# Order of the attention tiles, one mask ahead and the others among its steps

## Chip, cores and metric

The kernel runs on one core of a Trainium2 chip. The metric is the device time of one execution in microseconds (us), as the median of several runs.

## What is computed

One layer of a hybrid decoder trunk on x of 1024 positions and 1024 channels, all in float32. The reference, cut to what matters here:

```python
h = rmsnorm(x, norm_g) * (1 + scale) + shift          # shift, scale, gate from c
xr, gr, q, k, v, ga, qi, ki, wi = split(h @ w_in)
y_r = rg_lru(conv(xr), ...) * silu(gr)                # recurrence, 512 channels
# attention, 8 heads of 64, in blocks of 128 queries, one shared key and value:
score = sum_h relu(qi_h . ki / 8) * wi_h / sqrt(8)    # the indexer
score = where(causal, score, -inf)
idx = top_k(score, 256)                               # keys that a query may use
p = softmax(where(in idx and causal, q . k / 8, -inf))
y_a = (p @ v) * silu(ga)
x = x + gate * (concat(y_r, y_a) @ w_out)
return rmsnorm(x, final_g)
```

## The kernel before

**Early part.** TensorE projects h in 23 tiles of w_in (each product in three passes of high and low halves), while the other engines do the recurrence and the indexer's scores. Then, for query tiles 7 to 2 (tiles 0 and 1 have no more than 256 keys), the 256th largest score of each row is sought, a bit at a time in 31 rounds. Tile i has 128 (i + 1) keys. ScalarE counts for tiles 7, 6, 5 (columns c = 0, 1, 2 of PICK), VectorE for tiles 4, 3, 2 (c = 3, 4, 5) and updates all candidates. The order of this part on each engine comes from a planner, stages(), with estimated costs; the search ends about when the last projections do.

**From search to mask.** `settle` on VectorE finishes the thresholds of c = 0, 1, 2: eight operations on three columns, a count over each of the three score rows (line 1238), and four more (to line 1245). Then `own_threshold` for c = 3, 4, 5. ScalarE compares each score row with its threshold (Sign, line 1008), in the order MASK_ORDER = 3, 4, 5, 0, 1, 2. `mask` on VectorE (lines 1253 to 1257) turns a comparison into a mask in bias_sb: find ties, a scan that ranks them, and three operations that choose and scale. Masks 3, 4, 5 are made ahead of the attention, masks 0, 1, 2 at its steps 1, 5, 9 (MASK_AT).

**Attention.** 64 steps g, one head each; the eight tiles come in the order ATT, eight steps a tile. One loop over g stands on each engine, and each engine works in its own program order:
- TensorE in step g: scores of step g (lines 1599, 1600) into PSUM pair 2 + g % 2, output pieces, at the tile's turn four transpositions of o_sb (line 1631), in odd steps the product of a pair of heads with the values (line 1643), the transpositions of the probabilities of step g-1 (line 1656), in even steps the fold (line 1665).
- VectorE: scaled scores plus mask and their row minimum into prob (line 1361), a mask where one is due, the evacuation of y (line 1375), ya_raw and ya_lo at a tile's turn (lines 1393, 1396), pt_lo of step g-1 (line 1404), o_sb of a pair (line 1418).
- ScalarE: ya_hi at the turn, pv (line 1033), pt_hi of step g-1 (line 1043), Exp of step g (line 1051), scaling and squares of finished rows (lines 1058, 1071), and wo_hi, one row block of w_out a step, from step WO_START (line 1079). yr_half makes the high half of the recurrence's output (line 1016).
- GpSimd: wo_lo (line 818), yr_lo (line 825), residual and final multiplications (lines 837 to 847).
- SyncE: loads of w_out as soon as the projections are done, then x_res and final_g, then out and in by tile.

There are three prob buffers. The minimum of step g waits for its scores and for the transpositions of step g-3.

**Output.** y of a tile is the product of its 1024 mixed channels with w_out: eight pieces a tile (line 1621, six products of 512 columns each), all into PSUM bank 3; after four pieces VectorE takes half a tile out. Piece 0 runs at step OUT_START = 20, two pieces in each of steps 20 to 26, then one a step: piece g - 13. Pieces 4k wait for the evacuation before (y_ok).

## Time and profile before

| what | value |
|---|---|
| median of 3 runs | 606.87 us (605.71 to 607.12) |
| the profiled execution: its time | 603.09 us |
| its span, first to last instruction | 601.3 us |
| TensorE busy | 531.6 us, 88% |
| VectorE busy | 429.7 us, 71% |
| ScalarE busy | 384.9 us, 64% |
| GpSimd busy | 211.3 us, 35% |
| mean granted TensorE clock | 0.949 of full speed |

The table is read from the page of the profile. Busy shares are means over stages that have different limits. PE is TensorE's products, PEld its loading of weights beside them, DVE is VectorE, ACT ScalarE, POOL GpSimd, SP SyncE. Times in rows count from the first instruction. A granted clock of 1.00 is 2.4 GHz and one of 0.50 is 1.2 GHz.

### The profile page before, as it was taken

Reading aid. Unit: us, or ns where it says so; the run is one execution under the profiler, and the core shown is the slowest. Engines: PE = TensorE matmul, PEld = TensorE weight load, DVE = VectorE, ACT = ScalarE, POOL = GpSimd, SP = SyncE. Lnnn points to the kernel's source line nnn. Section 1 sums busy time; section 2 is a strip of 40 time slices with the busy share of each in tenths; the row PEclk is TensorE's granted clock in tenths of the full one; section 3 lists DMA queues with packets and bytes.
Section 4 is the critical chain, followed back from the end, with each engine's and each line's share of the span. In section 5 each row is a group of like instructions: output and inputs, shape, how many; then the busy total and the mean of one; then the engine's idle time right before and its main releaser. Section 6 shows DMA issues by size and latency. Waiting matters only on the chain.

```text
span 601.3 us, 8070 instructions
## 1 busy us (share of the span) xinstructions
PE 531.6 (88%) x2676; PEld 441.5 (73%) x2676; DVE 429.7 (71%) x990; ACT 384.9 (64%) x683; POOL 211.3 (35%) x186
## 2 busy tenths in 40 slices
PE   0489988999999999999999527789999999999994
PEld 0467767888687777778888426678898999888873
DVE  4784659798989889997897886564566756655532
ACT  4583543554699999988897544773666665656530
POOL 6422062032345355497552000681322030413322
PEclk9999998999999999999999855599999999999998
DMA  8992393041111121134561330200201020101011
GB/s 301 396 348 77 74 293 101 23 106 35 37 35 36 37 67 38 36 106 106 131 152 35 136 144 0 92 14 2 71 1 70 1 71 1 70 1 71 1 70 71
DMA packets 19658, 51.98 MB, mean 86 GB/s; under 512 B 4128, under 2 KB 5152, under 8 KB 19616
## 3 DMA queue, kind: packets, MB, share of 16 engines
q1 hardware_dynamic: 19616, 51.45, 27.1%
q8 instruction: 22, 0.36, 0.3%
q14 instruction: 20, 0.16, 0.1%
HBM read 37.81 MB, written 4.19 MB: 70 GB/s over the span
## 4 chain that ended last, share of the span: by engine, by line
PE 69%; DVE 14%; ACT 7%; issue 5%; POOL 2%; DMA 2%; SPq 1%; DVEq 0%; POOLq 0%; ACTq 0%
PE pair L1496 26%; PE pair L1621 13%; PE pair L1643 6%; PE pair L1656 5%; PE pair L1465 4%; PE pair L1599 2%; PE pair L1573 2%; PE pair L1600 2%; PE pair L1665 2%; DVE score_sb L1325 2%; DVE rank L1254 2%; PE pair L1564 1%; PE pair L1565 1%; PE pair L1442 1%; DMA x_sb<-in_x 1%
## 5 line engine op out<-in xcount | busy, mean ns | idle before, releaser
L1404 DVE TENSOR_TENSOR pt_lo<-pair,pt_hi 128x512 fp32r<-128x512 f32 (+3 forms) x96 | 50.5, 554 | 71.7 <-ACT pt_hi L1043 71.2
L1496 PE MATMUL pair<-h_hi,w_hi 128*128 128x512 f32 x304 | 98.3, 405 | 0.0
L938 ACT ACTIVATE bias_sb<-score_sb,tinies 128x1024 bf16<-128x1024 f32 (+2 forms) x93 | 95.7, 1031 | 3.2 <-DVE tinies L1207 3.1
L1496 PE MATMUL pair<-h_lo,w_hi 128*128 128x512 f32 x304 | 94.4, 392 | 0.0
L1496 PE MATMUL pair<-h_hi,w_lo 128*128 128x512 f32 x304 | 93.7, 389 | 0.0
L1193 DVE TENSOR_SCALAR_CACHE_REDUCE bias_sb<-score_sb,tinies 128x640 bf16<-128x640 f32 (+2 forms) x93 | 72.4, 801 | 0.8
L746 POOL TENSOR_SCALAR w_hi<-w_raw 128x1024 fp32r<-128x1024 f32 (+1 forms) x22 | 23.6, 1075 | 135.0 <-DMA w_raw<-in_w_tiles 115.3
L1496 PEld LDWEIGHTS pair<-h_hi,w_hi 128*128 128x128 f32 x304 | 56.5, 189 | 14.5 <-issue 4.5
L1496 PEld LDWEIGHTS pair<-h_lo,w_hi 128*128 128x128 f32 x304 | 57.4, 189 | 12.4
L1496 PEld LDWEIGHTS pair<-h_hi,w_lo 128*128 128x128 f32 x304 | 57.3, 188 | 12.2
L1043 ACT ACTIVATE pt_hi<-pair 128x512 fp32r<-128x512 f32 (+3 forms) x96 | 43.5, 488 | 25.8 <-PE pair L1656 23.4
L837 POOL TENSOR_TENSOR x_res<-q_free,x_res 128x512 f32<-128x512 f32 x14 | 18.1, 1296 | 111.3 <-DVE q_free L1375 111.3
L955 ACT ACTIVATE relu<-pair 128x1024 f32<-128x1024 f32 (+5 forms) x48 | 34.3, 757 | 35.4 <-PE pair L1565 18.0
L1325 DVE SCALAR_TENSOR_TENSOR score_sb<-relu,tinies,score_sb 128x1024 f32<-128x1024 f32 (+5 forms) x42 | 43.5, 1077 | 7.8 <-ACT relu L955 7.8
L1656 PE MATMUL pair<-ident,prob 128*128 128x128 f32 x194 | 30.8, 287 | 18.4 <-ACT prob L1051 18.4
L1643 PE MATMUL pair<-pt_hi,v_pair 128*128 128x256 f32 x144 | 39.0, 304 | 5.0 <-DVE o_sb L1418 3.6
L1599 PE MATMUL pair<-key_hi,qs 128*128 128x512 f32 (+3 forms) x96 | 40.6, 424 | 0.0
L818 POOL TENSOR_TENSOR wo_lo<-wo_raw,wo_hi 128x1024 fp32r<-128x1024 f32 x8 | 18.7, 2364 | 59.9 <-ACT wo_hi L1079 59.9
L1656 PEld LDWEIGHTS pair<-ident,prob 128*128 128x128 f32 x194 | 23.3, 145 | 22.0 <-issue 15.8
L1033 ACT ACTIVATE pv<-pair 128x256 f32<-128x256 f32 x32 | 12.2, 380 | 39.6 <-PE pair L1643 39.5
L1643 PE MATMUL pair<-pt_lo,v_pair 128*128 128x256 f32 x144 | 37.4, 293 | 0.0
L1051 ACT ACTIVATE prob<-prob,tinies 128x256 f32<-128x256 f32 (+7 forms) x43 | 33.4, 776 | 2.8 <-DVE tinies L1361 2.8
(204 smaller groups left out, 1306.6 us busy)
## 6 DMA issues: line engine op xcount, KB each, us to landing
w_raw<-in_w_tiles SPq DMA_DIRECT2D x21, 512.0 KB, 3.8
ada<-in_ada_w SPq DMA_DIRECT2D x16, 512.0 KB, 12.1
x_sb<-in_x SPq DMA_DIRECT2D x8, 512.0 KB, 9.1
ada_g<-in_ada_w SPq DMA_DIRECT2D x8, 512.0 KB, 6.3
qs<-half_hi SPq DMA_DIRECT2D x16, 256.0 KB, 3.8
...
```

What stands on the lines that cost most here:

```text
L938: nc.scalar.activation(junk[i], score_sb[:, SCORE_OFF[i]:SCORE_OFF[i] + keys_of(i)], ACT.Sign, bias=cand[:, c:c + 1], scale=-1.0, accum_ou ...
L955: nc.scalar.activation(relu_sb[relus % 2][:, 0:n], pairs[PAIR["idx", o[1]]][:, 0:n], ACT.Relu, scale=HD ** -0.5).then_inc(slot_free, 1)
L1043: nc.scalar.activation(pt_hi[:, 4 * b:4 * b + nc4, hh, :], psum[use % 2][:, 0:nc4 * P].rearrange("p (c q) -> p c q", q=P), ACT.Copy).then_ ...
L1051: nc.scalar.activation(prob_of(g)[:, 0:n], prob_of(g)[:, 0:n], ACT.Exp, bias=negmax[:, g % 3:g % 3 + 1], scale=-1.0, accum_out=rsum[:, g % ...
L1193: nc.vector.tensor_scalar(junk[PICK[c]], scores(c), cols(c, cand), cols(c, nK), ALU.is_ge, ALU.add, accum_out=cols(c, cnt)).then_inc(count ...
L1325: nc.vector.scalar_tensor_tensor(dst, src, w, dst, ALU.mult, ALU.add).then_inc(summed, 1)
L1404: nc.vector.tensor_tensor(pt_lo[:, 4 * b:4 * b + nc4, hh, :], psum[use % 2][:, 0:nc4 * P].rearrange("p (c q) -> p c q", q=P), f32(pt_hi[:, ...
L1496: ins = nc.tensor.matmul(psum[banks[half]][0:width, :], w[b][:, k, 0:width], hh[:, k, half * HALF:(half + 1) * HALF], start=(k == 0 and p ...
L1599: nc.tensor.matmul(dst, qs[:, h, i * P:(i + 1) * P], key_hi[:, c:c + w], start=True, stop=False)
L1621: ins = nc.tensor.matmul(bank(3), y, w[:, m, half * HALF:(half + 1) * HALF], start=(m == 0 and p == 0), stop=(m == KC - 1 and p == 2))
L1643: ins = nc.tensor.matmul(psum[2][:, 0:256], v_pair[:, c, :], t[:, c, :, :].rearrange("p h q -> p (h q)"), start=(c == 0 and p == 0), stop= ...
L1656: ins = nc.tensor.transpose(psum[use % 2][:, (c % 4) * P:(c % 4 + 1) * P], prob_of(g - LAG_T)[:, c * P:(c + 1) * P], ident[:, :])
```

## The change

The tiles are taken in the order 4, 3, 2, 1, 0, 7, 6, 5. Only the mask of tile 4 is made ahead of the attention. `mask` is split into `ranks` and `biases`, and the halves stand at steps 1 and 2 (tile 3), 9 and 11 (tile 2), 16 to 21 (tiles 7, 6, 5). The settling of the thresholds of tiles 7, 6, 5 moves from before the own thresholds to steps 4 (`settle`) and 6 (`settle_counts`), and their comparisons on ScalarE to steps 8 to 10. An Exp of one element is put on ScalarE ahead of the first comparison. wo_hi starts at step 2 instead of 10, the output pieces at step 14 instead of 20 (two pieces in step 14 alone, then one a step), so the last piece stays at step 76. The prob buffers are two instead of three, and the minimum of step g waits for the transpositions of step g-2. x_res is loaded after three masks instead of six, final_g after 8 steps instead of 16. The square's by-product goes into yg, and the evacuation of y waits for the square of the tile before instead of the residual addition. Ties and ranks of tiles 7, 6, 5 lie over the scores of tile 7. Zeros for the scan and two small operands move to other PSUM banks, which brings the waits on TensorE.

```diff
-ATT = [1, 0, 4, 7, 6, 5, 3, 2]
+ATT = [4, 3, 2, 1, 0, 7, 6, 5]
...
-MASK_AT = {4 * c + 1: c for c in range(ACT_COLS)}
-WO_START = 10
-OUT_START = 20
+MASK_ORDER = (3, 4, 5, 0, 1, 2)
+RANK_AT = {1: 4, 9: 5, 16: 0, 18: 1, 20: 2}
+BIAS_AT = {2: 4, 11: 5, 17: 0, 19: 1, 21: 2}
+SETTLE_AT = (4, 6)
+CMP_AT = {8: 0, 9: 1, 10: 2}
+YR_AT = 11
+ZERO_AT = 12
+WO_START = 2
+OUT_START = 14
...
-    add("DVE", ("post",), 5.0, 4, *[("update", SEARCH_BITS - 1, c) for c in range(ACT_COLS)])
-    add("DVE", ("own_thr",), 0.3, 4, ("own", SEARCH_BITS - 1))
...
+    add("DVE", ("own_thr",), 0.3, 0, ("own", SEARCH_BITS - 1))
+    for n, c in enumerate(MASK_ORDER[:ACT_COLS]):
+        add("ACT", ("cmp", c), 0.5 + keys_of(PICK[c]) / 1200, 5, ("own_thr",), *[("cmp", b) for b in MASK_ORDER[:n]])
...
-            tie[i] = sb(f"tie{i}", R_S + 4 * SCORE_OFF[i], [P, keys_of(i)], BF16)
-            rank[i] = sb(f"rank{i}", R_S + 4 * SCORE_OFF[i] + 2 * keys_of(i), [P, keys_of(i)], F16)
+            at = R_S + 4 * SCORE_OFF[i if i in PICK[ACT_COLS:] else PICK[0]]
+            tie[i] = sb(f"tie{i}", at, [P, keys_of(i)], BF16)
+            rank[i] = sb(f"rank{i}", at + 2 * keys_of(i), [P, keys_of(i)], F16)
...
-        fg_bc = q_free[:, :, 0:P]
-        yg = [q_free[:, 4 * n:4 * n + 4, P:2 * P] for n in range(2)]
+        fg_bc = q_free[:, :, ATT[0] * P:ATT[0] * P + P]
+        yg = [q_free[:, 4 * n:4 * n + 4, ATT[1] * P:ATT[1] * P + P] for n in range(2)]
...
-            return (prob[0], prob[1], prob_late if g >= 16 else prob_early)[g % 3]
+            return prob[g % 2]
...
-            sp.wait_ge(bias_ok, len(PICK))
+            sp.wait_ge(bias_ok, len(PICK) - ACT_COLS)
...
-            sp.wait_ge(att_ps, 16)
+            sp.wait_ge(att_ps, 8)
...
+                    if o[1] == MASK_ORDER[0]:
+                        nc.scalar.activation(warm[:, :], ones[:, :], ACT.Exp)
                         act.wait_ge(own_thr_ok, 1)
...
-                if g == OUT_START - 4:
-                    act.wait_ge(bias_ok, len(PICK))
+                if g == YR_AT:
+                    act.wait_ge(bias_ok, 1)
+                    act.wait_ge(compared, len(PICK))
                     yr_half(0)
                     yr_half(1)
...
+                if g in CMP_AT:
+                    act.wait_ge(thr_ok, 2)
+                    compare(CMP_AT[g])
...
-                    nc.scalar.activation(sq_junk, x_res[ti % 2][:, half * HALF:(half + 1) * HALF], ACT.Square,
+                    xs = x_res[ti % 2][:, half * HALF:(half + 1) * HALF].rearrange("p (c q) -> p c q", q=P)
+                    nc.scalar.activation(yg[half], xs, ACT.Square,
...
+            def ranks(c):
...
+                dve.wait_ge(compared, MASK_ORDER.index(c) + 1)
+                if c < ACT_COLS:
+                    dve.wait_ge(bias_ok, MASK_ORDER.index(c))
                 link(nc.vector.tensor_scalar(tie[i][:, :], t, 0.0, None, ALU.is_equal))
+                link(nc.vector.tensor_tensor_scan(rank[i][:, :], tie[i][:, :], zero.to_broadcast([P, n]), float(n - 2 * TOPK), ALU.add, ALU.add))
+
+            def biases(c):
...
                 link(nc.vector.tensor_scalar(cols(c, nK), rank[i][:, n - 1:n], cols(c, cnt), 0.5, ALU.subtract, ALU.mult))
                 link(nc.vector.scalar_tensor_tensor(tie[i][:, :], rank[i][:, :], cols(c, nK), t, ALU.is_gt, ALU.is_gt))
                 nc.vector.tensor_scalar(t, tie[i][:, :], BIG, None, ALU.mult).then_inc(bias_ok, 1)
...
+            dve.wait_ge(evac_done, len(EVAC))
+            link(nc.vector.memset(zeros[0], 0.0))
+            ranks(MASK_ORDER[0])
+            biases(MASK_ORDER[0])
             dve.wait_ge(bias01_ok, 2)
...
-                    if g == 16:
-                        dve.wait_ge(bias_ok, len(PICK))
+                    if i in PICK and g % 8 == 0:
+                        dve.wait_ge(bias_ok, MASK_ORDER.index(PICK.index(i)) + 1)
                     dve.wait_ge(att_ps, g + 1)
-                    if g >= 3:
-
-                        dve.wait_ge(t_ps, last_t(g - 3) + 1)
+                    if g >= 2:
+                        dve.wait_ge(t_ps, last_t(g - 2) + 1)
...
-                if g in MASK_AT:
-                    mask(MASK_AT[g])
+                if g == SETTLE_AT[0]:
+                    settle()
+                if g == SETTLE_AT[1]:
+                    settle_counts()
+                if g == ZERO_AT:
+                    link(nc.vector.memset(zeros[1], 0.0))
+                if g in RANK_AT:
+                    ranks(RANK_AT[g])
+                if g in BIAS_AT:
+                    biases(BIAS_AT[g])
...
-                        dve.wait_ge(x1_ok, 2 * (ti - 1) + half + 1)
+                        dve.wait_ge(sq1_ok, 2 * (ti - 1) + half + 1)
...
+                    if g == 1:
+                        pe.wait_ge(own_thr_ok, 1)
+                    if g % 8 == 0 and i == PICK[0]:
+                        pe.wait_ge(bias_ok, len(PICK))
...
+                    if o == 0:
+                        pe.wait_ge(bias_ok, len(PICK) - ACT_COLS)
+                        pe.wait_ge(thr_ok, 2)
```

## Rows read from the trace of the kernel before

**Rows 1.** The page: granted TensorE clock in 40 slices of the span.

```profile
PEclk9999998999999999999999855599999999999998
```

**Rows 2.** Busy time by stage: window, length, then busy us (instructions) of each engine.

```profile
339.00:353.00 14.00, 0.66 (x5) 0.42 (x3) 12.33 (x28) 6.88 (x13) 0.00 (x0) 0.60 0.78 300
353.00:394.00 41.00, 28.96 (x118) 25.33 (x119) 27.67 (x82) 24.40 (x68) 12.23 (x6) 0.51 0.12 39
549.00:569.30 20.30, 19.66 (x120) 16.92 (x118) 11.41 (x35) 12.13 (x32) 6.03 (x7) 1.00 0.08 28
```

**Rows 3.** The chain that ended last: start, us, engine, tile, line.

```profile
402.03 2.85 PE pair L1621 x12
...
446.10 1.37 PE pair L1621 x6
...
449.38 0.87 PE pair L1656 x8
...
454.80 1.37 PE pair L1621 x6
...
481.44 1.66 PE pair L1643 x14
...
489.49 1.66 PE pair L1643 x14
...
588.24 5.76 PE pair L1621 x24
```

**Rows 4.** Timeline of TensorE: start, us, instruction, and the idle time before it.

```profile
355.26 0.66 PE L1656 MATMUL pair<-ident,prob 128*128 128x128 f32 x2 [15.61 <-ACT prob L1051]
```

**Rows 5.** Timeline of VectorE: settling, first masks, first minimum, a mask of 1024 keys.

```profile
338.64 1.34 DVE L1238 TENSOR_SCALAR_CACHE_REDUCE bias_sb<-score_sb,tinies 128x1024 bf16<-128x1024 f32 x1
...
342.14 0.16 DVE L1241 SCALAR_TENSOR_TENSOR tinies<-tinies 128x3 f32<-128x3 f32 x1
...
344.24 0.33 DVE L1253 TENSOR_SCALAR tie<-bias_sb 128x640 bf16<-128x640 bf16 x1 [1.08 <-ACT bias_sb L1008]
...
347.54 0.29 DVE L1253 TENSOR_SCALAR tie<-bias_sb 128x512 bf16<-128x512 bf16 x1
...
352.72 0.42 DVE L1361 CUSTOM_DVE_ANT_0 prob<-pair,bias_sb 128x256 f32<-128x256 f32 x1
...
353.40 0.42 DVE L1253 TENSOR_SCALAR tie<-bias_sb 128x1024 bf16<-128x1024 bf16 x1
...
358.09 0.42 DVE L1404 TENSOR_TENSOR pt_lo<-pair,pt_hi 128x256 fp32r<-128x256 f32 x1
```

**Rows 6.** Timeline of ScalarE: last projection, comparison, table load, two pt_hi.

```profile
339.22 1.03 ACT L919 ACTIVATE ga<-pair 128x1024 f32<-128x1024 f32 x1 [3.71 <-PE pair L1496]
343.20 0.92 ACT L1008 ACTIVATE bias_sb<-score_sb,tinies 128x640 bf16<-128x640 f32 x1 [2.95 <-DVE tinies L1221]
...
353.22 1.28 ACT L1051 ACT_TABLE_LOAD   x1 [4.17 <-DVE tinies L1361]
354.52 0.51 ACT L1051 ACTIVATE prob<-prob,tinies 128x256 f32<-128x256 f32 x1
...
394.61 0.76 ACT L1043 ACTIVATE pt_hi<-pair 128x512 fp32r<-128x512 f32 x2
...
397.00 0.77 ACT L1043 ACTIVATE pt_hi<-pair 128x512 fp32r<-128x512 f32 x2
```

**Rows 7.** Timeline of VectorE: ya_lo of two tiles.

```profile
382.32 1.26 DVE L1396 TENSOR_TENSOR ya_lo<-ya_raw,ya_hi 128x512 fp32r<-128x512 f32 x1 [0.69 <-ACT ya_hi L1027]
...
580.39 0.69 DVE L1396 TENSOR_TENSOR ya_lo<-ya_raw,ya_hi 128x512 fp32r<-128x512 f32 x1 [0.70 <-ACT ya_hi L1027]
```

**Rows 8.** Timeline of GpSimd: seven wo_lo in a row.

```profile
384.13 16.34 POOL L818 TENSOR_TENSOR wo_lo<-wo_raw,wo_hi 128x1024 fp32r<-128x1024 f32 x7 [1.09 <-ACT wo_hi L1079]
```

**Rows 9.** TensorE in two short windows: length, busy us (instructions), granted clock, DMA.

```profile
362.50:365.90 3.40, 3.26 (x15) 0.50 0.00 0
389.80:393.20 3.40, 3.40 (x13) 0.51 0.51 152
```

48 lines of the change are left out of this document (17 added, 31 removed).

## Prediction, made before the change was built

> **What bounds the kernel now.** I read the clock line of the page first, because a whole stretch of it is below full speed [rows 1]: the TensorE clock is at nines up to slice 22, at five for three slices, and at nines again. The busy shares by stage [rows 2] say what lies there. From 339 to 353 us TensorE is busy for 0.66 of 14 us and VectorE for 12.3: VectorE settles the search and makes masks. From 353 to 394 us TensorE is busy for 29.0 of 41 us at a granted clock of 0.51, that is at 1.2 of its 2.4 GHz. These are the steps of tiles 1 and 0, with hardly any work in each and no output pieces (those start at step 20). In the chain [rows 3] the first output piece runs at 402.0, the last ends at 588.24 + 5.76 = 594.0, and nearly all between is TensorE; 7.3 us of closing work follow to 601.3. So there are two regimes: until 402.0 waits and a half clock set the time, afterwards TensorE's own work does. A change is worth what it takes from the first 62 us, less what it puts into the other 192.
>
> **The start.** The first transposition runs at 355.26, after 15.61 us without work on TensorE [rows 4]. In these lie the settling, 338.64 to about 343, three masks in a row from 344.24, and the first softmax minimum at 352.72 [rows 5]; then ScalarE's table load of 1.28 us and an Exp [rows 6]. After the change the mask of tile 4 comes first, alone. The last projection is moved out of PSUM at 339.22 + 1.03 = 340.2 [rows 6] and VectorE waits for that. ScalarE then does the warming Exp: the load of 1.28 and, as an estimate, 0.2 for one element, to 341.7. From the start of a comparison of 640 keys to the start of its mask the trace has 343.20 to 344.24, 1.04; the mask takes 344.24 to 347.54, 3.3 [rows 5, 6]. The first minimum so starts at 346.0 instead of 352.7. It and the Exp are longer (640 keys, about 0.8 and 0.9, for 256 keys' 0.4 and 0.5), but the load no longer lies in the path: first transposition at 348.0, 7.3 us earlier. The Trainium skill (ScalarE: Activation LUTs, What ACT_TABLE_LOAD costs) gives 2.66 us for a switch, load and drain together. The trace has the Exp 0.02 us behind the 1.28, so I use 1.28; by the page all of this would come 1.4 us later.
>
> **Steps 0 to 13.** These steps now belong to tile 4 and most of tile 3. Prices at full clock [rows 3]: eight transpositions 0.87, so 0.109 each; fourteen products with the values 1.66, so 0.119 each. At half clock they double. Of tile 7's pair of heads (8.70, below) two pieces, sixteen transpositions and sixteen products leave 2.3 for the scores and the fold; for 640 keys I put 1.6, so 0.8 a step and 1.6 at half clock. With five transpositions (1.1) and half of a pair's ten products (1.2), one step of tile 4 is 3.9 us of TensorE at half clock.
> - Steps 0 to 2: both parts of the mask of tile 3 (2.8, on the line of the masks below) between three minima and the first waits for Exp and transposition: 7.6 us, to 353.6.
> - Steps 3 to 5: TensorE's 3.9 each, and small waits as the pipe fills, for which I allow 1.6: 13.3, to 366.9. The eight tiny settling operations at step 4 are hidden in this.
> - Step 6: the counts of the settling take 338.64 to 342.14, 3.5, and the operations behind them 0.6 [rows 5]. They stand between the minimum and pt_lo of step 5, which the values' product waits for, and behind that the transposition. Three of the tiny operations read two operands in SBUF while GpSimd makes wo_lo. For that I go by ya_lo: 1.26 while GpSimd is at work, 0.69 when it isn't [rows 7], so 0.57 each, 1.7. (A wo_lo itself takes 16.34 / 7 = 2.33 [rows 8].) With the minimum, pt_lo and o_sb (2.2) the step is 8.0, to 374.9.
> - Steps 7 to 10: ScalarE goes from one pt_hi to the next in 394.61 to 397.00, 2.39, with an Exp of 640 keys and one wo_hi in it [rows 6]. To this come the comparisons of tiles 7, 6 and 5 at steps 8 to 10 (1.2, 1.1, 1.0, in proportion to the one above), and what the half clock adds to transposition and product ahead: 3.7 each, 14.8, to 389.7.
> - Steps 11 to 13: the last mask part of tile 2 (1.1), two yr_hi, and the turn of the first tile (TensorE, VectorE, ScalarE, VectorE): 7.8. The first piece starts at 397.5, now in step 14.
>
> The third prob buffer goes for nothing: the minimum of step g needs its scores, and TensorE issues those behind the transpositions of step g-2, so the new wait is over before the old one. Nor does wo_lo hold the pieces up: with the last wo_hi at step 9 and 2.33 us for each wo_lo it is done before step 12. The earlier loads of x_res and final_g land well before step 16, where they are first read. The y evacuation waits for a square eight steps back; nothing is queued there. If that cover were gone, each would cost a square, 0.6.
>
> **From the first piece on.** Before: 402.0 to 594.0, 192.0 us. The 64 pieces are the same. The attention work left at that point isn't. A pair of heads takes 454.80 - 446.10 = 8.70 for tile 7 and 489.49 - 481.44 = 8.05 for tile 6 [rows 3], so 0.65 less for each tile down; two pieces of 1.37 come off: 4.01 for tile 4, 3.36 for tile 3, 2.06 and 1.41 for tiles 1 and 0. Before, two pairs of tile 4 and all of 7, 6, 5, 3, 2 are left. After, one pair of tile 3 and all of 2, 1, 0, 7, 6, 5. The difference is 2 x 4.01 + 3 x 3.36 - 4 x 2.06 - 4 x 1.41 = 4.2 us less. Against it, the masks of tiles 7, 6 and 5 now stand in steps 16 to 21, those of tile 2. One of 1024 keys takes 353.40 to 358.09, 4.69 [rows 5]; on the line to the 3.30 for 640 keys the other two are 4.2 and 3.8, 12.7 in all. The other work of VectorE in these steps is 11.4 in seven steps of tile 2 in the row 549.0 to 569.3 [rows 2], so 9.8 in six, and 0.7 of wait in the turn: 23.2. TensorE has 6 x 2.72 and 0.4, 16.8. VectorE becomes the bound there and adds 6.4. In these steps the y evacuation also stands behind a mask part, and the next piece needs its bank, so the pieces cannot run ahead.
>
> **Sum.** 397.5 + 192.0 - 4.2 + 6.4 = 591.7, and 7.3 behind it: 599.0 against 601.3, 2.3 us less. The profiled execution took 603.09; the runs shown have a median of 606.87, 3.8 more, so I put the same difference on that: 604.6.
>
> **The clock** is the open point of this sum. It rose at 393.2. In 389.8 to 393.2, the row ahead, TensorE was busy for all 3.40 us; in 362.5 to 365.9, where it was busy for 3.26, it didn't rise [rows 9]. After the change TensorE runs with few gaps from step 3 on and then stands for six us at step 6. I take it that the clock is at half until that stop and up again at about 383, in a stretch of products without a gap.
>
> **Rivals.**
> - *Clock up early, and through the stop.* Then steps 7 to 13 lose the extra of transposition and product, and the first piece starts at about 395.5: 2.0 less than in the sum, 4.3 less than before, 602.6. For it: tile 4 has twice the work of tile 1 in a step. Against it: six us without work ahead. 0.18.
> - *The clock stays at half until the pieces.* This is the case on the other side. Steps 10 to 13 then take 3.3 us more and the first pieces run at 1.2 GHz for 2 more: 5.3 on the sum, 3.0 slower than before, 609.9. It decides (more than 0.3% slower) when the low clock costs over 4.1, about when it lasts to the first piece. For it: the whole of 353 to 394 in the trace. 0.20.
> - *The masks hide behind the pieces.* Then the 6.4 go: 8.7 less than before, 598.2. For it: TensorE has 1.4 us more in each step than without pieces. Against it: VectorE's sum alone is over TensorE's. 0.06.
> - *VectorE is shut out while GpSimd runs.* A blocked operation then waits for the whole of a wo_lo: three times 2.33 instead of three times 0.57, 5.3 more: 3.0 slower, 609.9. For it: GpSimd gets a wo_lo in each of those steps. Against it: ya_lo lost 0.57 only. 0.08. The Trainium skill (SBUF — State Buffer, Who interferes with whom) has this rule: an operation of VectorE with two SBUF inputs and one of GpSimd that reads SBUF exclude each other for a whole instruction.
> - *Sign is not in the table that Exp uses.* Eight more loads of 1.28, 10.2: 614.8. Before, Sign ran behind Silu without a load. 0.02.
>
> **How the numbers follow.** The case of the sum has 0.46. No change within 0.3% is 1.8 us either way, about what can be told here. My step times may be off by 4 us, so of its 0.46 I give 0.24 to faster, 0.17 to same and 0.05 to slower. The early clock and the hidden masks are faster (0.24); the late clock and the shut-out are slower but for 0.04, and the tables are slower: faster 0.48, same 0.21, slower 0.31. Range: below it takes in the hidden masks' edge, 598.5; above the late clock and 1 us, 611. The likeliest case alone has 601 to 609.
>
> **What would show it.** The first minimum at 346; a table load ahead of the first comparison and none behind it; a gap of TensorE of five to six us at about 368 to 374; the first piece near 397.5 at full clock; TensorE with gaps of about 1 us a step for some 23 us behind it and VectorE full there; then pairs of 8.7 and 8.05 again in tiles 7 and 6; 7.3 us of end. I am wrong if tile 0's steps with pieces are bound by the round through ScalarE and take much over 2.1 us, or if the clock falls again.

## The result, and the profile after

The changed kernel takes 616.31 us (median of 4 runs, 611.33 to 617.34) beside 606.29 for the kernel before (4 runs, 603.57 to 607.12): ratio 1.0157, 95% interval 1.0093 to 1.0221. It is slower by about 10 us, where 604.6 was forecast. The profiled execution took 616.18 us, its span is 614.4.

The page's clock line of the kernel after, beside [rows 1]: the three fives are gone, but seven slices in a row are below nine there, where before it was four.

```profile
PEclk9879979999999999999999777678899999999998
```

Busy time by stage of the kernel after (window, length, then us and instructions of TensorE, its weight loads, VectorE, ScalarE, GpSimd, then granted clock, DMA share and GB/s):

```profile
340.00:354.50 14.50, 6.25 (x26) 5.22 (x24) 9.86 (x22) 8.95 (x20) 0.00 (x0) 0.66 0.73 290
354.50:405.80 51.30, 36.17 (x161) 31.21 (x162) 30.04 (x74) 29.59 (x62) 21.42 (x10) 0.67 0.09 31
405.80:446.10 40.30, 34.32 (x183) 29.50 (x182) 27.98 (x61) 17.48 (x44) 7.21 (x7) 0.91 0.03 12
446.10:487.10 41.00, 37.86 (x223) 31.64 (x222) 18.33 (x74) 21.54 (x71) 14.29 (x14) 1.00 0.12 41
487.10:607.10 120.00, 117.29 (x725) 102.86 (x723) 69.43 (x143) 67.50 (x139) 27.47 (x27) 1.00 0.11 40
```

The last row, tiles 7, 6 and 5, is full of TensorE's work, as everything behind the first piece was before. The first four rows, 147.1 us, hold 32.5 us in which TensorE has nothing. The head of the chain of waits (start, us, engine, tile, line):

```profile
340.00 1.03 ACT ga L916
341.04 1.28 ACT L1005
342.34 0.20 ACT tinies L1005
342.54 0.91 ACT bias_sb L943 x2
343.55 0.34 DVE tie L1262
...
347.06 0.82 DVE prob L1374
347.98 0.93 ACT prob L1050 x2
...
349.05 1.10 PE pair L1684 x4
```

The start is as forecast: the warming Exp takes its load of 1.28 us ahead of the comparison, the mask of tile 4 starts 1.01 us behind the comparison, the first minimum is at 347.06 and the first transposition at 349.05; the last two are 1.1 us later than forecast, 0.8 of it because the last projection is (340.00, not 339.22 [rows 6]). Behind the load the next operation again follows by 0.02 us, so the 2.66 us of the Trainium skill (ScalarE: Activation LUTs, What ACT_TABLE_LOAD costs) aren't seen here either.

Then it parts. Here is the timeline of VectorE, and under it that of GpSimd, of the kernel after (start, us, line, tile out<-in, idle before):

```profile
361.15 1.88 DVE L1238 TENSOR_SCALAR tinies<-tinies 128x3 int32<-128x3 int32 x1
...
373.49 1.68 DVE L1247 SCALAR_TENSOR_TENSOR tinies<-tinies 128x3 f32<-128x3 f32 x1
375.21 0.16 DVE L1248 TENSOR_TENSOR tinies<-tinies 128x3 f32<-128x3 f32 x1
...
394.98 1.37 DVE L1272 TENSOR_SCALAR bias_sb<-tie 128x384 bf16<-128x384 bf16 x1
```
```profile
360.64 4.76 POOL L815 TENSOR_TENSOR wo_lo<-wo_raw,wo_hi 128x1024 fp32r<-128x1024 f32 x2 [2.73 <-ACT wo_hi L1082]
...
370.41 4.75 POOL L815 TENSOR_TENSOR wo_lo<-wo_raw,wo_hi 128x1024 fp32r<-128x1024 f32 x2 [5.00 <-ACT wo_hi L1082]
...
394.95 2.53 POOL L822 TENSOR_TENSOR yr_lo<-yr,yr_hi 128x512 fp32r<-128x512 f32 x2 [0.56 <-ACT yr_hi L1014]
```

An operation on three columns takes 0.16 us when nothing is beside it, and 1.88 or 1.68 here. The ends tell why: 361.15 + 1.88 = 363.03, and the first of GpSimd's two instructions ends at 360.64 + 2.38 = 363.02; 373.49 + 1.68 = 375.17, and the second of the next two ends at 375.16; 394.98 + 1.37 = 396.35, and the first half of yr_lo ends at 396.22. VectorE stands until GpSimd's instruction is over. (On 384 columns the third one goes on for 0.13 us behind it; with GpSimd idle it takes 0.26.) TensorE pays for it (its timeline, idle time in brackets):

```profile
364.70 0.36 PE L1671 MATMUL pair<-pt_hi,v_pair 128*128 128x256 f32 x1 [3.17 <-DVE o_sb L1439]
...
376.91 0.55 PE L1671 MATMUL pair<-pt_hi,v_pair 128*128 128x256 f32 x1 [5.63 <-DVE o_sb L1439]
...
418.28 0.50 PE L1649 MATMUL pair<-wo_hi,yr_hi 128*128 128x512 f32 x1 [2.35 <-DVE q_free L1396]
...
435.42 0.50 PE L1649 MATMUL pair<-wo_hi,yr_hi 128*128 128x512 f32 x1 [1.91 <-DVE q_free L1396]
```

The last two are pieces that wait for the evacuation of the output half ahead, which stands behind a scan of a mask. And in tiles 1 and 0 a new wait appears, in front of ScalarE's scaling of a finished tile (timelines of GpSimd and ScalarE in step 30):

```profile
460.44 1.30 POOL L822 TENSOR_TENSOR yr_lo<-yr,yr_hi 128x512 fp32r<-128x512 f32 x1 [1.36 <-ACT yr_hi L1014]
...
462.26 0.56 POOL L840 TENSOR_TENSOR tinies<-tinies 128x1 f32<-128x1 f32 x1
```
```profile
462.85 1.15 ACT L1060 ACTIVATE x_res<-x_res,tinies 128x1024 f32<-128x1024 f32 x1 [1.45 <-POOL tinies L840]
463.90 0.36 ACT L1042 ACTIVATE pt_hi<-pair 128x256 fp32r<-128x256 f32 x1
```

ScalarE can't scale before GpSimd has the row sums, these stand behind yr_lo, and pt_hi of the next transposition stands behind the scaling: 2.6 us. This step, 30, took 3.8 us, the two ahead of it 1.7 and 2.9.

The steps of all the kernels below, each tile's eight from minimum to minimum in the profiled execution (the first tiles in the order of the change; us):

| kernel | first minimum | tile 4 | tile 3 | tile 2 | tile 1 | tile 0 | first piece | end of last piece |
|---|---|---|---|---|---|---|---|---|
| after | 347.1 | 34.7 | 32.5 | 31.8 | 21.0 | 20.0 | 405.75 | 607.1 |
| stop_split | 346.6 | 31.2 | 30.3 | 32.1 | 21.0 | 20.0 | 399.7 | 601.2 |
| hold_clock | 347.6 | 30.4 | 28.5 | 30.5 | 21.0 | 20.0 | 398.0 | 597.9 |
| wo_around | 347.4 | 28.8 | 30.4 | 31.7 | 21.0 | 20.1 | 398.05 | 599.4 |
| y_first | 348.3 | 34.7 | 31.2 | 28.6 | 20.9 | 20.0 | 404.7 | 603.8 |
| finish_later | 348.9 | 34.3 | 30.3 | 32.1 | 19.4 | 18.4 | 405.15 | 603.4 |
| heavy_all | 347.2 | 30.6 | 31.1 | 28.2 | 19.5 | 18.4 | 400.56 | 595.0 |
| heavy_around | 347.6 | 29.2 | 29.7 | 28.2 | 19.5 | 18.4 | 398.07 | 592.6 |
| heavy_tuned | 349.3 | 25.4 | 27.8 | 28.9 | 19.5 | 18.4 | 393.99 | 589.3 |

Tiles 7 and 6 take 33.3 and 33.0 in all of them, within 0.1. Each row is one profiled execution. Ratios below are to the kernel before and leave out executions more than 1.5% above a kernel's fastest, which only three kernels had, all with repeated products: 4 of 12 of before_fill (614.7 to 618.0 us), 1 of 12 of heavy_all (1046.4) and 5 of 6 of light_all (625.2 to 627.1), each at a lower mean clock than its others.

The change's own four executions span 611.33 to 617.34 us, and the interval of its ratio overlaps those of stop_split, wo_around, finish_later and y_first below. What these four gain is therefore read from their steps. But steps, too, move with the clock from one execution to the next: steps 12 and 13 took 7.4 us in the change and in masks_out, with the clock at half for 7.0 and 6.7 us of them, and 5.7 in finish_later at full clock, though its edit lies behind them.

### The profile page after: what moved, and what is told of

Same layout as the page of the kernel before. It is cut to its first block, busy times and chain, and to the rows that moved or that the text cites. A ratio compares the mean times of both kernels' runs of the same rounds, so it can differ in the third digit from the quotient of the medians.

```text
span 614.4 us, 8087 instructions
## 1 busy us (share of the span) xinstructions
PE 544.0 (89%) x2676; PEld 450.5 (73%) x2676; DVE 429.4 (70%) x991; ACT 385.5 (63%) x684; POOL 208.9 (34%) x186
## 4 chain that ended last, share of the span: by engine, by line
PE 69%; DVE 12%; ACT 8%; issue 5%; POOL 3%; DMA 2%; SPq 1%; DVEq 0%; POOLq 0%; ACTq 0%
PE pair L1517 28%; PE pair L1649 11%; PE pair L1671 7%; PE pair L1684 5%; PE pair L1486 4%; PE pair L1594 2%; PE pair L1624 2%; PE pair L1625 2%; PE pair L1585 2%; PE pair L1586 2%; DVE score_sb L1336 1%; PE pair L1693 1%; DVE rank L1263 1%; PE pair L1463 1%; ACT pt_hi L1042 1%
## 5 line engine op out<-in xcount | busy, mean ns | idle before, releaser
L1517 PEld LDWEIGHTS pair<-h_hi,w_hi 128*128 128x128 f32 x304 | 56.9, 190 | 14.8 <-issue 4.7
L1517 PEld LDWEIGHTS pair<-h_hi,w_lo 128*128 128x128 f32 x304 | 57.4, 189 | 12.3
L1042 ACT ACTIVATE pt_hi<-pair 128x512 fp32r<-128x512 f32 (+3 forms) x96 | 43.5, 488 | 28.2 <-PE pair L1684 26.6
L1684 PE MATMUL pair<-ident,prob 128*128 128x128 f32 x288 | 48.4, 301 | 13.8 <-ACT prob L1050 13.6
L960 ACT ACTIVATE relu<-pair 128x1024 f32<-128x1024 f32 (+5 forms) x48 | 34.3, 757 | 35.5 <-PE pair L1586 23.6
L1671 PE MATMUL pair<-pt_hi,v_pair 128*128 128x256 f32 x144 | 42.8, 323 | 12.4 <-DVE o_sb L1439 12.1
L1684 PEld LDWEIGHTS pair<-ident,prob 128*128 128x128 f32 x288 | 37.6, 154 | 21.1 <-ACT prob L1050 10.7
L1050 ACT ACTIVATE prob<-prob,tinies 128x640 f32<-128x640 f32 (+7 forms) x64 | 49.6, 775 | 3.0 <-DVE tinies L1374 3.0
L1374 DVE CUSTOM_DVE_ANT_0 prob<-pair,bias_sb 128x640 f32<-128x640 f32 (+7 forms) x64 | 47.9, 749 | 0.8 <-PE pair L1625 0.4
L1671 PEld LDWEIGHTS pair<-pt_hi,v_pair 128*128 128x128 f32 x144 | 31.5, 219 | 16.0 <-DVE pt_lo L1425 15.4
L1671 PE MATMUL pair<-pt_lo,v_pair 128*128 128x256 f32 x144 | 41.4, 314 | 0.0
```

The source lines that it names most:

```text
L1042: nc.scalar.activation(pt_hi[:, 4 * b:4 * b + nc4, hh, :], psum[use % 2][:, 0:nc4 * P].rearrange("p (c q) -> p c q", q=P), ACT.Copy).then_ ...
L1050: nc.scalar.activation(prob_of(g)[:, 0:n], prob_of(g)[:, 0:n], ACT.Exp, bias=negmax[:, g % 3:g % 3 + 1], scale=-1.0, accum_out=rsum[:, g % ...
L1374: nc.vector.tensor_tensor_reduce(out=prob_of(g)[:, 0:n], in0=pairs[2 + g % 2][:, 0:n], in1=bias_sb[:, BIAS_OFF[i]:BIAS_OFF[i] + n], scale= ...
L1517: ins = nc.tensor.matmul(psum[banks[half]][0:width, :], w[b][:, k, 0:width], hh[:, k, half * HALF:(half + 1) * HALF], start=(k == 0 and p ...
L1671: ins = nc.tensor.matmul(psum[2][:, 0:256], v_pair[:, c, :], t[:, c, :, :].rearrange("p h q -> p (h q)"), start=(c == 0 and p == 0), stop= ...
L1684: ins = nc.tensor.transpose(psum[use % 2][:, (c % 4) * P:(c % 4 + 1) * P], prob_of(g - LAG_T)[:, c * P:(c + 1) * P], ident[:, :])
```

## The experiments

**Masks left out (masks_out).** The ranks and biases of tiles 7, 6 and 5 are left out; these tiles use the raw comparison as bias.

```
                 if g in RANK_AT:
-                    ranks(RANK_AT[g])
+                    if RANK_AT[g] >= ACT_COLS: ranks(RANK_AT[g])
                 if g in BIAS_AT:
-                    biases(BIAS_AT[g])
+                    if BIAS_AT[g] >= ACT_COLS: biases(BIAS_AT[g])
+                    else: (two memsets of one column, the second counting bias_ok)
```

> The changed kernel without the mask work of tiles 7, 6 and 5: ranks and biases of these are left out at steps 16 to 21, so these tiles use what the comparison left. Theory masks: the eight steps of tile 2 took 31.8 us where before they took about 23; they fall to 23, and 8 to 9 us go, to about 608. Theory that only what goes beyond TensorE's work counts (6.4 as predicted): about 610. If the clock's falls in these steps are what costs, they are gone too and 10 us or more go.

Measured 607.03 us, ratio 1.0021 (0.9995 to 1.0046). Tile 2's steps fall from 31.8 to 22.9 us, all else stays. The three masks cost 8.9 us beside TensorE's pieces; I had forecast 6.4. In the change the clock also falls to half twice in these steps, for 3.4 us each (419.7 and 436.8), and in masks_out it doesn't: what that costs is within the 8.9.

**One count a step (stop_split).** The settling is put at step 3, its three counts at steps 4, 5 and 6.

```
-SETTLE_AT = (4, 6)
+SETTLE_AT = (3, 4)
-                for c in range(ACT_COLS):
+                for c in (g - SETTLE_AT[1],):
+                if c < ACT_COLS - 1: return
```

> The changed kernel with the settling at step 3 and its three counts one each at steps 4, 5 and 6, with the closing operations behind the third. Theory stop (a single block of 4 us on VectorE makes TensorE idle for 5.6 and lets the clock fall): 3 to 5 us go, to about 612. Theory sum (VectorE's work in the head counts, wherever it stands): no change within 1 us, 616.

Measured 611.48 us, ratio 1.0111 (1.0079 to 1.0142); the first piece comes at 399.7, 6 us earlier. But step 6, now with one count in place of three, still took 7.1 us (7.4): the operations behind the counts took 1.62 and 2.35 us there. So 2.4 us of counts went out of step 6, and 2.1 us of standing beside GpSimd came in. The gain lies elsewhere: 3.3 us in steps 3 to 5, and 1.7 in steps 12 and 13, where its clock was at full. These 1.7 are in finish_later too, so they are not the split's.

**The clock held (hold_clock).** Score products are repeated to the same place, so that TensorE isn't idle.

```
+FILL_AT = {1: 10, 3: 1, 5: 4, 7: 7, 9: 1, 11: 4, 13: 2}
-                    for c in range(0, n, HALF):
+                    for c in [*range(0, n, HALF)] * (1 + FILL_AT.get(g, 0)):
```

> The changed kernel with the score products of steps 1, 3, 5, 7, 9, 11 and 13 repeated (10, 1, 4, 7, 1, 4, 2 times more, the same result), so that TensorE is at work where it stood idle. Theory clock: the granted clock stays at 1.0 from 341 to the first piece, transpositions and products halve there, and the first piece comes 5 to 8 us earlier: about 609. Theory rounds (the head is bound by VectorE and ScalarE): the clock is at 1.0, but no more than 2 us go.

Measured 608.94 us, ratio 1.0064 (1.0035 to 1.0092). The row of hold_clock from its first minimum to its first piece, and under it that of after, both with the clock in the third column from the end:

```profile
347.60:398.00 50.40, 38.27 (x247) 32.45 (x246) 36.73 (x88) 33.02 (x70) 21.62 (x10) 1.00 0.19 71
```
```profile
347.10:405.80 58.70, 41.15 (x179) 35.45 (x180) 36.55 (x88) 33.63 (x71) 21.42 (x10) 0.65 0.16 60
```

At full clock the stretch is 8.3 us shorter, although TensorE gets 68 instructions more, as the theory of the clock had it.

**The same in the kernel before (before_fill).**

```
+FILL_AT = {1: 60, 2: 2, 3: 5, 4: 2, 5: 4, 6: 2, 7: 5, 8: 4, 9: 3, 10: 4, 11: 7, 12: 8, 13: 4, 14: 4, 15: 4}
```

> The kernel before with the score products of its steps 1 to 15 repeated (the same operands to the same place; 60 extra times at step 1, where TensorE is idle 15.6 us, 2 to 8 times at the others), and nothing else. Theory A (the half clock of 342.2 to 393.2 is a cost of the light tiles: their transpositions, folds and products lie in the round of a step and take 0.25 to 0.45 us more in it): the granted clock stays 1.0 from 342 to the end, the 16 light steps fall from 38.4 to about 33 us, the whole to 600. Theory B (the light steps are bound by VectorE and ScalarE and the clock costs nothing there): the steps stay at 38 and the whole within 0.3% of the kernel before, or above it by what the repeats add.

Measured ratio 0.9993 (0.9967 to 1.0018). The row of its sixteen light steps:

```profile
354.60:392.20 37.60, 30.55 (x233) 28.56 (x231) 26.74 (x77) 20.64 (x61) 8.32 (x4) 0.95 0.08 29
```

The clock was at 0.95 in place of 0.51 [rows 2], and the steps took 37.6 us in place of 38.4. My expectation of 33 was wrong. But the repeats were in the way too. In the timeline of VectorE minima wait for the repeated products (line 1601), here the three longest of five:

```profile
356.00 0.42 DVE L1362 CUSTOM_DVE_ANT_0 prob<-pair,bias_sb 128x256 f32<-128x256 f32 x1 [0.94 <-PE pair L1601]
...
364.71 0.42 DVE L1362 CUSTOM_DVE_ANT_0 prob<-pair,bias_sb 128x256 f32<-128x256 f32 x1 [0.38 <-PE pair L1601]
...
367.32 0.42 DVE L1362 CUSTOM_DVE_ANT_0 prob_early<-pair,bias_sb 128x256 f32<-128x256 f32 x1 [0.94 <-PE pair L1601]
```

These waits are 2.6 us in all; in the kernel before none of the sixteen minima waits for TensorE, and in hold_clock one does, for 0.28. So under tiles 1 and 0 the half clock costs 0.8 us as measured, and by my estimate up to 3.4, if all these waits hid a gain; under tiles 4 and 3 the low clock costs over 8.

**Two prob buffers alone (two_prob),** in the kernel before.

```
-            return (prob[0], prob[1], prob_late if g >= 16 else prob_early)[g % 3]
+            return prob[g % 2]
-                    if g >= 3:  dve.wait_ge(t_ps, last_t(g - 3) + 1)
+                    if g >= 2:  dve.wait_ge(t_ps, last_t(g - 2) + 1)
```

> The kernel before with two prob buffers in place of three, with the wait on the transpositions two steps back, and nothing else. Theory A (the third buffer is never what lets a minimum start): the whole within 0.3% of the kernel before, 604.5 to 608, and each tile's steps within 0.3 us of the kernel before. Theory B (the two buffers are a cost of the change, since each minimum now waits for the transposition two steps back): 2 us or more slower, with the minima waiting on the transpositions in the light tiles 1 and 0 above all.

Measured 605.83 us, ratio 1.0007 (0.999 to 1.0024): the third buffer goes for nothing, as forecast. One of A's marks was missed: the steps of tile 4 took 32.0 us, not within 0.3 of the 31.0 before; the clock was at half until 399.6 there, before until 393.1.

**The light tiles first (light_first).** The settling in parts and the masks among the steps, as in the change, in the order of tiles before.

```
-ATT = [4, 3, 2, 1, 0, 7, 6, 5]
+ATT = [1, 0, 4, 7, 6, 5, 3, 2]
+RANK_AT = {4: 3, 6: 4, 7: 5, 9: 0, 11: 1, 13: 2}
+BIAS_AT = {5: 3, 7: 4, 8: 5, 10: 0, 12: 1, 14: 2}
+SETTLE_AT = (0, 1)     # one count a step
+CMP_AT = {5: 0, 6: 1, 7: 2}
+OUT_START = 15
```

No mask is made ahead of the attention, and within a step `biases` stands ahead of `ranks`.

> The changed kernel with the tiles in the order of before (1, 0, 4, 7, 6, 5, 3, 2). Since tiles 1 and 0 need no mask, the first minimum no longer waits for one; settling, counts and all mask halves stand one or two a step in steps 0 to 14; pieces start at step 15. Theory order (heavy tiles stand where nothing covers the round through the engines, light ones beside pieces): the first minimum comes near 341.5, the first piece near 388, with all masks made; about 590 to 596 us, faster than before. Theory masks (it is the halves among the steps that cost, wherever they stand): steps 0 to 14 take as long as steps 0 to 13 did after the change, and the time stays over 606.

Measured 606.35 us, ratio 1.0016 (0.9995 to 1.0036): 10 us better than the change, but no better than the kernel before, and 10 short of what I expected. The first minimum came at 343.3 (341.5 expected), the first piece at 395.3 (388). The first sixteen steps took 57.6 us.

**The round of a finished tile later (finish_later).**

```
-                if ti + 2 < NT: split_yr(ti + 2)     # GpSimd, ahead of the row sums
...
+                if ti + 2 < NT: split_yr(ti + 2)     # GpSimd, behind them
-                for o in PIECES.get(g - 1, ()):
+                for o in PIECES.get(g - 2, ()):      # ScalarE's scale
```

> The changed kernel with the round of a finished tile put later: GpSimd splits the recurrent half of the tile after next behind the three small operations on the row sums and not ahead of them, and ScalarE scales the finished row block two steps after its last piece and not one. Theory A (the steps of tiles 1 and 0 are bound by the round through ScalarE and GpSimd, in which the scale waits 1.45 to 1.65 us in front of the copies that the transpositions need): step 38 to 39 falls from 3.7 to about 2.5 us, the turn steps 27 and 35 too, tiles 1 and 0 from 21.0 and 20.0 to 18.5 and 17.5 us, and the other turns of tiles 7 to 5 stay, since they have a slack; the whole 611.5 us (4 to 6 less than the changed kernel's 616.3). Theory B (those steps are bound by TensorE's own work and the wait of ScalarE is slack): tiles 1 and 0 stay at 21.0 and 20.0 and the whole within 1 us of 616.3.

Measured 612.83 us, ratio 1.012 (1.009 to 1.0149); tiles 1 and 0 take 19.4 and 18.4 us, 3.2 less together, where A had 5. The same place in its timeline of ScalarE:

```profile
461.46 0.38 ACT L1042 ACTIVATE pt_hi<-pair 128x256 fp32r<-128x256 f32 x1 [0.60 <-PE pair L1684]
461.75 0.50 ACT L1050 ACTIVATE prob<-prob,tinies 128x256 f32<-128x256 f32 x1
...
462.24 1.14 ACT L1060 ACTIVATE x_res<-x_res,tinies 128x1024 f32<-128x1024 f32 x1
```

The scaling no longer waits and stands behind pt_hi. The turn steps 27 and 35 stay at 3.7 and 3.8: they are the first tile's way through four engines, which the row sums have no part in.

**The evacuation first (y_first).** In VectorE's step:

```
+                for o in PIECES.get(g, ()):     # evacuation of an output half, moved here
                 if g == SETTLE_AT[0]:
                     settle()
...
                     biases(BIAS_AT[g])
-                for o in PIECES.get(g, ()):
```

> The changed kernel with VectorE's evacuation of an output half moved ahead of the settling and the masks in the step. Theory A (the 8.9 us that the three masks cost in the steps of tile 2 come in part from pieces that wait on an evacuation behind a scan: TensorE is idle 2.35 us at 418.3 and 1.91 us at 435.4 for it): steps 16 to 23 fall from 31.8 to about 28.5 us, the whole to 613. Theory B (VectorE's own work is the sum, in whatever order: the masks take 3 x 4.7 us on VectorE and the cost is what exceeds its idle time): the steps stay at 31.8 within 0.7 us, since the next minimum now waits behind evacuation and scan as before, and the whole stays at 616 within 1 us.

Measured 613.26 us, ratio 1.0134 (1.0103 to 1.0165). By the whole alone that is no safe difference from 1.0157; by the steps it is: tile 2 takes 28.6 us in place of 31.8, as A had it. So up to 3.2 of the masks' 8.9 us were pieces that waited for a bank behind a scan. Part of it is the clock: y_first has one fall in tile 2 where the change has two, and hold_clock, with no edit there and one fall, took 30.5, which leaves about 1.8 to the order alone.

**The weights split later (wo_later).**

```
-WO_START = 2
+WO_START = 6
```

> The changed kernel with the splitting of the output weights begun at step 6 in place of step 2, so that GpSimd is idle while the search's result is settled and until the counts. Theory A (two of VectorE's tiny operations took 1.88 and 1.68 us in place of 0.17 and 0.16 because GpSimd was working on the output weights): both fall under 0.3 us, the first comparison mask's later op takes 1.4 again or more, since it now lies beside GpSimd's work as well, the steps 4 to 6 together fall by about 3 us (17.2 to 14.2), and the first output piece comes no earlier than the last of the eight halves, so near 403 to 406; whole 613 to 616. Theory B (the long operations come from what stands ahead of them on VectorE or from the clock): their times stay at 1.9 and 1.7 us.

Measured 620.61 us, ratio 1.0248 (1.0209 to 1.0288). The answer for the one line and the timelines of VectorE and GpSimd:

```profile
L1238 DVE TENSOR_SCALAR tinies<-tinies x1: 169/169/169, 361.1 to 361.1; 128x3 int32<-128x3 int32 x1
```
```profile
370.52 1.59 DVE L1247 SCALAR_TENSOR_TENSOR tinies<-tinies 128x3 f32<-128x3 f32 x1
```
```profile
369.75 2.34 POOL L815 TENSOR_TENSOR wo_lo<-wo_raw,wo_hi 128x1024 fp32r<-128x1024 f32 x1 [47.20 <-ACT wo_hi L1082]
```

L1238, with GpSimd idle, is back at 0.169 us. L1247 met the first wo_lo, now at 369.75, and again ended with it: 370.52 + 1.59 = 372.11, 369.75 + 2.34 = 372.09. That is neither theory's letter (A wanted both short) but A's mechanism twice. L1238 reads a single tensor, so the rival of my prediction, which spoke of two SBUF inputs, did not cover it. Steps 4 and 5 fell by 2.9 us; the end was lost to step 14, 12.2 us long, since yr_lo, behind the last wo_lo, was done at 406. It is the rule of the Trainium skill that I had given 0.08 (SBUF — State Buffer, Who interferes with whom): the later of the two blocks fully until the first finishes.

**All four edits (heavy_all):** stop_split, hold_clock, y_first and finish_later together.

> The changed kernel with the four edits that each took something off it: one count a step from step 4 (4.8 us less by itself), the repeated score products that hold the clock (7.4), the evacuation of an output half ahead of settling and masks (3.1), the round of a finished tile later (3.5). If they add up: 616.3 less 18.8, 597.5, faster than the kernel before by 1.3%. If the first two overlap, since both shorten the stretch in which the counts stand (full clock also shortens the transpositions behind them): 600 to 603. Over 604: the parts do not add and the order of tiles 4, 3, 2, 1, 0, 7, 6, 5 itself is the cost.

Measured 604.32 us, ratio 0.9976 (0.996 to 0.9992): 12 of the 18.8 us came. VectorE and GpSimd at step 6:

```profile
368.88 1.66 DVE L1250 SCALAR_TENSOR_TENSOR tinies<-tinies 128x3 f32<-128x3 f32 x1
370.57 2.36 DVE L1251 TENSOR_TENSOR tinies<-tinies 128x3 f32<-128x3 f32 x1
```
```profile
368.11 4.80 POOL L816 TENSOR_TENSOR wo_lo<-wo_raw,wo_hi 128x1024 fp32r<-128x1024 f32 x2 [3.25 <-ACT wo_hi L1083]
```

Two operations, two instructions of GpSimd back to back, 370.5 and 372.9 their ends.

**The splitting laid around the settling (wo_around),** in the changed kernel, nothing else:

```
-                if WO_START <= g < WO_START + KC:  m = g - WO_START
+                for m in WO_AT.get(g, ()):
+WO_AT = {2: [0], 4: [1], 5: [2], 7: [3], 8: [4], 9: [5], 10: [6], 11: [7]}
```

> The changed kernel with the eight splittings of the output weights laid around the settling: at steps 2, 4, 5, 7, 8, 9, 10 and 11 in place of 2 to 9, so that GpSimd has no instruction under way when the settling's tiny operations at steps 4 and 6 start. Theory A (a tiny VectorE operation with its operands in SBUF that starts while GpSimd works stands until GpSimd's instruction ends: 361.15 + 1.88 = 363.03 against 360.64 + 2.38, and 373.49 + 1.68 = 375.17 against 370.41 + 4.75): the two fall to 0.16 and 0.17 us, steps 4 and 6 get 1.7 and 1.5 us shorter, and the whole is 613 (3.2 less than 616.3) if the splitting's end, now at step 11, does not hold the first piece. Theory B (the 1.9 and 1.7 us lie beside other waits that take their place): they fall, but the steps 4 and 6 keep within 0.5 us of 5.0 and 7.4, and the whole stays at 616.

Measured 610.28 us, ratio 1.0079 (1.0051 to 1.0107), more than A's 3.2. All the tiny operations take 0.15 to 0.17; steps 3 to 6 take 3.6, 3.3, 3.6 and 5.9 us in place of 5.0, 5.0, 4.8 and 7.4, and the first piece comes at 398.05. Not all of it is the edit's: the clock was up at 354.1, just ahead of step 3, and at 358.2 in the change, though the two kernels do the same until then. The steps take the two causes apart. hold_clock, with the blocked operations in place and the clock at full, has 3.6 us at steps 3 and 5 as well, but 5.0 and 7.5 at steps 4 and 6. So the blocks cost steps 4 and 6 together 3.2 us, as A had it, and the half clock cost steps 3 and 5 together 2.6.

**The four edits with the splitting laid around (heavy_around).** WO_AT = {3: [0], 4: [1], 7: [2], 8: [3], 9: [4], 10: [5, 6], 11: [7]}.

> The changed kernel with the four edits of the experiment that joined them (604.3 us) and the splitting of the output weights at steps 3, 4, 7, 8, 9, 10 (two) and 11 in place of 2 to 9. In that experiment three tiny operations of the settling took 2.16, 1.66 and 2.36 us, each to the end of an instruction of GpSimd. Theory A (the four edits did not add up because the counts' split moved the settling's last part onto two such instructions, 3.7 us): step 6 falls from 7.2 to about 3.5 us and the whole to 598 to 600, about 1% faster than the kernel before. Theory B (step 6 is long for another reason): it stays over 5.5 us and the whole at 603 to 605.

Measured 601.73 us, ratio 0.9938 (0.9914 to 0.9961), less than A. The operations at 368.7 took 0.16, but step 6 still 6.8:

```profile
373.60 0.82 DVE L1376 CUSTOM_DVE_ANT_0 prob<-pair,bias_sb 128x640 f32<-128x640 f32 x1 [3.20 <-PE pair L1627]
```

The minimum waits for scores: the seven repeats at step 7 had been sized for a stall that was gone. And at step 11 a subtraction for ya_lo met the doubled wo_lo and took 2.79 us.

**The repeats cut to fit (heavy_tuned).** FILL_AT = {1: 10, 3: 1, 5: 1, 7: 1, 9: 1, 11: 3, 13: 1}, WO_AT one a step at 3, 4 and 6 to 11.

> The changed kernel with the four edits and the splitting around the settling (601.7 us), with fewer repeated products (at step 7 one in place of seven, at 5 one in place of four, at 11 three in place of four) and the splitting one a step at 3, 4 and 6 to 11. There step 6 stayed at 6.8 us although the settling's last part took 0.5 us: VectorE sat idle 3.2 us for score products, whose repeats had been sized for the stall that was gone; step 11 took 7.5 us, 2.8 of them a subtraction beside GpSimd. Theory A (both are only that): step 6 falls to 3.5 us, step 11 to 5.5, the whole to 597 to 599, if the clock still holds. If the clock falls to half for want of repeats: 600 to 603.

Measured 597.1 us (6 runs, 595.94 to 598.37), ratio 0.9859 (0.9826 to 0.9891). Its row from the first minimum to the first piece:

```profile
349.30:394.00 44.70, 32.64 (x209) 27.45 (x207) 32.94 (x88) 32.94 (x70) 20.46 (x10) 0.96 0.22 80
```

Step 6 takes 3.5 us, tile 4 25.4 in place of 34.7; the stretch is 44.7 us long in place of 58.7, at a clock of 0.96. It is the fastest kernel of this study, 9 us under the kernel before and 19 under the change, in the change's own order of tiles.

**The light order, its splitting laid around too (light_around and light_late).** WO_AT = {1: [0], 14: [1], ... 20: [7]}; OUT_START = 21, then 24.

> The kernel of the experiment with the light tiles first (606.4 us) and the splitting of the output weights at steps 1 and 14 to 20 in place of 2 to 9, the first output piece at step 21 in place of 15. There some ten operations of settling and masks stood 1 to 2.4 us longer than their like beside GpSimd's instructions, 9 to 10 us in all. Theory A (that is the bound of the head, with VectorE its busiest engine): steps 0 to 15 fall from 57.6 to 50 us, the later pieces give back 1 to 3 us between steps 16 and 32, the whole 600 to 603. Theory B (the head is bound by the masks' own work and the pieces' place matters more): steps 0 to 15 stay over 55 us and the whole is 606 to 612.

> The kernel of the experiment with the light tiles first and the weights' splitting around the masks (607.1 us), with the first output piece at step 24 in place of 21. There the head of 16 steps took 44.8 us in place of 57.6, and the end came at the same time, because TensorE sat idle 5.2 us for the first piece and the steps around it took 12.3 us. Theory A (behind step 16 the order with light tiles first is bound by TensorE's own work, some 196 us, which was busy 28.6 of 28.6 and 34.3 of 34.3 us there; what the head saves is kept if no piece is asked for before GpSimd has its operands): the last piece comes at about 589 in place of 597, the whole 597 to 599, faster than the kernel before by 1.2 to 1.5%. Theory B (pieces put off come back as TensorE's time in the heavy tiles, since it has no idle time left there): the end stays at 597 and the whole at 605 to 607.

light_around: 607.1 us, ratio 1.0027 (1.0008 to 1.0047). light_late: 603.5 us, ratio 0.9963 (0.9942 to 0.9984). The first sixteen steps of light_first and of light_around, and TensorE of light_around at the first piece:

```profile
343.30:400.90 57.60, 29.65 (x119) 25.59 (x120) 47.63 (x109) 30.21 (x79) 22.49 (x10) 0.56 0.27 100
```
```profile
341.80:386.60 44.80, 26.39 (x107) 23.10 (x108) 37.85 (x108) 25.18 (x74) 4.72 (x2) 0.52 0.34 129
```
```profile
405.19 0.77 PE L1646 MATMUL pair<-wo_hi,yr_hi 128*128 128x512 f32 x1 [5.15 <-POOL yr_lo L822]
```

VectorE is busy 9.8 us less with the same work, and the head is 12.8 us shorter. In light_around it is given back whole: tile 4 takes 36.0 us for 28.6, with 12.3 in step 21, and tile 7 41.2 for 34.4. In light_late it is given back mostly, though no piece waits like that: its two stages behind the head, tiles 4 and 7, are

```profile
388.00:412.60 24.60, 18.64 (x124) 16.86 (x123) 16.03 (x42) 19.05 (x42) 16.71 (x8) 0.94 0.00 1
412.60:457.80 45.20, 45.20 (x269) 39.78 (x268) 24.52 (x48) 22.70 (x46) 9.67 (x9) 1.00 0.07 24
```

and in the first of them TensorE has 6 us free with no pieces to fill them, in the second none. The whole, 603.5, lies between A (597 to 599) and B (605 to 607), nearer to B: in this order the pieces put off come back as TensorE's time.

**Everything in the light order (light_all):** light_first with repeats at steps 1 to 15 (28 and 30 at steps 9 and 11), y_first and finish_later.

> The kernel of the experiment with the light tiles first (tiles 1, 0, 4, 7, 6, 5, 3, 2, the settling and five of the masks among the steps), with three more edits: score products repeated in steps 1 to 15 to hold the clock, VectorE's evacuation of an output half ahead of settling and masks, and the round of a finished tile put later on GpSimd and ScalarE. If the parts are independent: 606.4, less about 5 for the clock, less 1 to 3 for the two others: 598 to 601, a version faster than both kernels by about 1%. If the light order's head is bound by VectorE's settling and masks and not by the clock, 604 to 606.

It tells nothing of the two other edits. The median is 625.33 us; one of six executions took 604.11, at a mean clock of 0.986, and the profiled one 625.42, at 0.940. In the profiled one the clock was at half from 365 to 420 with TensorE busy all the while,

```profile
365.00:420.00 55.00, 54.74 (x248) 53.73 (x249) 26.10 (x55) 11.26 (x34) 12.37 (x6) 0.50 0.09 29
```

and the steps 8, 10 and 11, in which the repeated scores of 9, 11 and 12 run, took 10.8, 13.8 and 9.5 us. I had sized a repeat of 128 columns at half of one of 256; they started 0.21 us apart there, each product as far as one of 256 columns does at that clock.

## Why the prediction was wrong

The sum had the first piece at 397.5 and 194.2 us from it to the end of the last. Measured: 405.75 and 201.3. The two misses, 8.2 and 7.1 us, are the whole difference between the span forecast, 599.0, and the measured 614.4.

- *The start*: right. First transposition 348.0 forecast, 349.05 measured; 0.8 of the 1.05 is the earlier part.
- *"The eight tiny settling operations at step 4 are hidden in this"*, and *"0.57 each"* for the others: the first step that failed. An operation of this kind that meets GpSimd's work doesn't lose a share; it stands until the instruction ends. The three that met one lost 1.7, 1.5 and 1.1 us; the first I had put at nothing, the second at 1.7 for three, of which only the first was hit (the other two took 0.16, GpSimd being done). The third, in a mask part at step 11, I hadn't thought of. Steps 3 to 5 took 14.8 us where I had 13.3. The rival that had this right had a chance of 0.08, because I read ya_lo's 1.26 [rows 7] as a slowdown by 0.57. It was what was left of a wo_lo, less 0.15; in the timeline of GpSimd of the kernel before it stands, had I laid the two side by side:

```profile
380.68 2.36 POOL L818 TENSOR_TENSOR wo_lo<-wo_raw,wo_hi 128x1024 fp32r<-128x1024 f32 x1 [58.80 <-ACT wo_hi L1079]
```

  It ended at 383.04, 0.72 behind ya_lo's start. The next ya_lo in that trace, at 401.07, lost 0.51 with 0.65 left of a yr_lo. wo_around moved GpSimd's work alone and took 1.7 us off step 4 and 1.5 off step 6.
- *"Up again at about 383"*: the second. The granted clock went to half (1.2 GHz) six times between 344 and 440 us instead, 51 us in all, as long as in one piece before; from the first minimum to the first piece it was 0.65 in the mean. Steps 7 to 10 took 16.8 us (14.8 forecast), steps 11 to 13 12.3 (7.8), the latter at half clock from 392 to 406. The rival *the clock stays at half until the pieces* put 3.3 us more on steps 10 to 13; they took 4.4 more, though the clock rose in between, so the price came about without the course that it described. With the clock held (hold_clock) the stretch from the first minimum to the first piece is 50.4 us, blocked operations and all, where the forecast had 51.5 and the change took 58.7. wo_around took 50.6, 3.2 of the gain by the blocks and 2.6 by the clock at steps 3 and 5. In heavy_tuned, with all these edits and fewer repeats, it is 44.7.
- *Step 6* at 8.0: 7.4 measured, and the counts 3.5 of it. The sum came near by luck: its last part had 1.7 us for three slowed operations, and one blocked operation lost 1.5.
- *"VectorE becomes the bound there and adds 6.4"*: mechanism right, size off: 8.9 (masks_out). Up to 3.2 of it are pieces behind a scan (y_first). I had written that the pieces can't run ahead there, and given that no price.
- *"2.06 and 1.41 for tiles 1 and 0"*: the last step that failed. With two pieces a pair that is 19.2 and 16.6 us for the tiles; they took 21.0 and 20.0. My line through tiles 7 and 6 is a price of TensorE; these steps are bound by the round through GpSimd and ScalarE. 3.2 of the 5.2 us come back with finish_later. The other 2 are the turns, as I take it; no run here shows it. It stood in the prediction among what would make it wrong.
- *"The third prob buffer goes for nothing"*: right (two_prob), and so was the cover of wo_lo: it held up no piece.

So the order of tiles doesn't bar a faster kernel: in the same order, heavy_tuned is 1.4% faster than the kernel before. It isn't a fair contest of the two orders, though. The kernel before has none of heavy_tuned's edits, and only the repeats were tried on it (before_fill, nothing gained); what an earlier evacuation or a later round would give it no run shows. The change moved GpSimd's splitting beside VectorE's smallest operations, put tiles that feel the low clock more where tiles that feel it less had been, and put tiles with little work beside pieces whose round through other engines is longer than they are. What stays open is the split of steps 7 to 15 between clock and waits, which hold_clock and wo_around each shorten and no run takes apart, and why the clock falls in one execution and not in another.
